# Eight convolution products per attention step in place of ten, and the first projection item begun in the last steps

## The reference

```python
def short_conv(u, b_gate, c_gate, w):
    z = jnp.pad(c_gate * u, ((0, 0), (CONV_W - 1, 0), (0, 0)))
    y = z[:, 0:s_len] * w[0]
    for i in range(1, CONV_W):
        y = y + z[:, i:i + s_len] * w[i]
    return b_gate * y

def hybrid_mixer(h, w_in, ...):
    z = h @ w_in                      # q, keys, values, gates, u, bg, cg
    ...
    o_attn = g[0] * o_cmp + g[1] * o_sel + g[2] * o_win    # 8 heads of 64
    o_conv = short_conv(u, bg, cg, conv_w)                 # 512 channels
    return jnp.concatenate([o_attn, o_conv], axis=-1) @ w_o

h = layer_norm(ALPHA * h + hybrid_mixer(h, ...), ln1_g[l], ln1_b[l])
```

## Time and profile before

| what | value |
|---|---|
| median of 3 runs | 2651.23 us (2649.49 to 2657.9) |
| profiled execution, its own time | 2649.5 us |
| its span, first to last instruction | 2647.6 us |
| mean granted clock of TensorE | 0.977 |
| TensorE busy | 2498.7 us, 94% |
| VectorE busy | 1392.4 us, 53% |
| ScalarE busy | 1035.5 us, 39% |
| steps 0 to 34 of mixer 2 | 1149.58 to 1290.48 us of the span |
| steps 0 to 34 of mixer 3 | 1821.95 to 1964.47 us of the span |

### The profile page before, as it was taken

The page is one execution under the profiler, slowest core; times in us unless marked ns, Lnnn a source line. Parts: engine busy times, 40 slices in busy tenths (PEclk is TensorE's granted clock), DMA queues, the critical chain, the costliest instruction groups (busy, mean ns, idle before and its releaser), DMA issues.

```text
span 2647.6 us, 37963 instructions
## 1 busy us (share of the span) xinstructions
PE 2498.7 (94%) x15190; PEld 2009.3 (76%) x15190; DVE 1392.4 (53%) x2043; ACT 1035.5 (39%) x1402; POOL 192.8 (7%) x136
## 2 busy tenths in 40 slices
PE   7999999998999999999999999998987999999993
PEld 5888888776788887877668888777765878887872
DVE  3433446465443345466463323456655666666666
ACT  4222233334322223345442212234544556555652
POOL 1000010000100002200130000220002000000000
PEclk9999999999999999999999999999998999999997
DMA  4232223201222221321112322222113677777773
GB/s 146 101 109 80 107 85 111 71 26 40 104 103 103 80 107 68 107 96 49 48 64 95 112 81 105 83 91 96 49 39 153 237 266 269 274 270 267 273 261 133
DMA packets 50752, 328.36 MB, mean 124 GB/s; under 512 B 5857, under 2 KB 5985, under 8 KB 19169
## 3 DMA queue, kind: packets, MB, share of 16 engines
q1 hardware_dynamic: 45184, 310.60, 32.5%
q0 software_dynamic: 4032, 13.88, 1.4%
q10 hardware_dynamic: 1440, 2.57, 0.3%
HBM read 317.58 MB, written 9.44 MB: 124 GB/s over the span
## 4 chain that ended last, share of the span: by engine, by line
PE 85%; DVE 7%; ACT 3%; DMA 2%; issue 2%; POOL 1%; ACTq 0%; DVEq 0%; SPq 0%; POOLq 0%
PE ps L2285 16%; PE ps L2286 16%; PE ps L2287 16%; PE ps L912 5%; PE ps L1515 3%; PE ps L1501 3%; PE ps L1516 3%; PE ps L1517 3%; PE ps L1558 2%; PE ps L1544 2%; PE ps L417 1%; PE ps L1560 1%; PE ps L1559 1%; PE ps L967 1%; PE ps L1002 1%
## 5 line engine op out<-in xcount | busy, mean ns | idle before, releaser
L2285 PE MATMUL ps<-xh,wh 128*128 128x512 f32 x1344 | 532.4, 396 | 37.3 <-DVE xl L2141 14.0
L2286 PE MATMUL ps<-xl,wh 128*128 128x512 f32 x1344 | 528.4, 393 | 0.0
L2287 PE MATMUL ps<-xh,wl 128*128 128x512 f32 x1344 | 528.2, 393 | 0.0
L1877 DVE TENSOR_TENSOR wl<-raw,wh 128x2048 fp32r<-128x2048 f32 (+3 forms) x137 | 330.1, 2410 | 151.5 <-ACT wh L1872 151.5
L1872 ACT CAST wh<-raw 128x2048 fp32r<-128x2048 f32 (+3 forms) x137 | 270.1, 1972 | 326.0 <-PE ps L2287 291.4
L1733 DVE TENSOR_TENSOR wml<-raw_m,wmh 128x2048 fp32r<-128x2048 f32 (+1 forms) x146 | 307.0, 2115 | 118.4 <-ACT wmh L1593 117.7
L2285 PEld LDWEIGHTS ps<-xh,wh 128*128 128x128 f32 x1344 | 256.1, 191 | 96.5 <-issue 23.9
L1593 ACT CAST wmh<-raw_m 128x2048 fp32r<-128x2048 f32 (+1 forms) x146 | 257.6, 1770 | 106.7 <-PE ps L1501 73.0
L2286 PEld LDWEIGHTS ps<-xl,wh 128*128 128x128 f32 x1344 | 255.8, 190 | 54.7 <-issue 1.5
L2287 PEld LDWEIGHTS ps<-xh,wl 128*128 128x128 f32 x1344 | 255.5, 190 | 53.9
L2285 PE MATMUL ps<-ah,wh 128*128 128x512 f32 x528 | 206.2, 391 | 0.0
(11 more groups left out here) (379 smaller groups left out, 3946.0 us busy)
## 6 DMA issues: line engine op xcount, KB each, us to landing
raw_m<-in_moe SPq DMA_DIRECT2D x104, 1024.0 KB, 5.2
raw<-in_ffn_up SPq DMA_DIRECT2D x65, 1024.0 KB, 4.8
raw_m<-in_moe SPq DMA_DIRECT2D x32, 768.0 KB, 4.2
raw<-in_in SPq DMA_DIRECT2D x20, 1024.0 KB, 4.9
raw<-in_ffn_down SPq DMA_DIRECT2D x12, 1536.0 KB, 6.5
raw<-in_ffn_down SPq DMA_DIRECT2D x12, 1280.0 KB, 5.3
raw<-in_cmp SPq DMA_DIRECT2D x8, 1024.0 KB, 4.7
raw<-in_out SPq DMA_DIRECT2D x8, 1024.0 KB, 4.7
```

Source lines behind the costliest of these rows:

```text
L1877: nc.vector.tensor_tensor(wl[:, slot, 0:size], raw[:, slot, 0:size], wh[:, slot, 0:size].bitcast(F32), ALU.subtract).then_inc(lo_ready, 1)
L2285: nc.tensor.matmul(dst, hi_w, hi_x, start=(k == 0), stop=False)
L2286: nc.tensor.matmul(dst, hi_w, lo_x, start=False, stop=False)
L2287: return nc.tensor.matmul(dst, lo_w, hi_x, start=False, stop=(k == last_k))
```

## The change

- DENSE is 8, so that the 240 products fill steps 0 to 29; chunk_end and all that is placed by it move with them.
- The convolution results are split one by one, ScalarE in steps 22, 25, 28 and 31 (chunk_end(8 + c) + 2), VectorE one step later each (23, 26, 29, 32), and go to the unused ends of the weight slots (conv_part) in place of xh and xl. ScalarE's wait for the last convolution item is gone.
- 15 of the 48 products of the projection's item 0 (units 0 to 4 of 16, three products each) are issued within the steps: one unit in step 30, one in 31, one in 32, two in 34, each time between the scores (where there are any) and the transposes. In step 30 a wait for the item's split weights (lo_ready) and for the evacuation of the last convolution item (evac_done) stands ahead of them. The other 33 follow the steps.
- Item j of the projection uses banks 0 and 1 for even j and 4 and 5 for odd j, in both mixers.

```diff
--- before.py
+++ after.py
@@ -58,7 +58,7 @@
 TILES = (0, 1, 2, 3)
 STEPS = 8 * NT
 STEPS1 = 4 * NT
-DENSE = 10
+DENSE = 8
 WIN = 4 * NCMP
 TILE = P * P // P
 UPS = 12
@@ -318,6 +318,11 @@
             "h_att", "h_masked", "h_turned", "h_ktok", "h_upd", "h_state", "h_out", "h_sq", "h_stat", "h_rstd", "h_rec"))
         MIX0 = split_base["mixed0"]
         MIXED_ORDER = (4, 5, 6, 7, 0, 1, 2, 3)
+        EARLY = ((30, 0, 1), (31, 1, 2), (32, 2, 3), (34, 3, 5))
+
+        def conv_part(w, c):
+
+            return w[:, c // 2, ITEM + (c % 2) * S:ITEM + (c % 2 + 1) * S]
         turned = reset
         x_free, qk_hi, qk_lo, p_half, p_evac, h_hi, h_lo = (sem(n) for n in (
             "x_free", "qk_hi", "qk_lo", "p_half", "p_evac", "h_hi", "h_lo"))
@@ -888,7 +893,7 @@
 
             return ((q - 2) * 24 + 23) // DENSE if q >= 2 else -1
 
-        def pe_mixer(pe, l):
+        def pe_mixer(pe, l, mixed_early):
             n0, nb = first[f"cmp{l + 1}"], first[f"conv{l + 1}"]
             u0, t0 = STEPS1 + STEPS * l, NT * l
 
@@ -1017,6 +1022,7 @@
                     scores(s)
                 for x in range(s * DENSE, min((s + 1) * DENSE, 240)):
                     conv(2 + x // 24, x % 24, x % 24 + 1)
+                mixed_early(l + 1, s)
                 if 0 <= s - 2 < STEPS:
                     turn(s - 2)
                 if 8 <= s < 12:
@@ -1116,10 +1122,10 @@
                             half_split(nb + k + 1, h)
                 if s >= 13 and (s - 13) % 8 == 0 or s == STEPS + 3:
                     out_hi((s - 11) // 8)
-                if 26 <= s < 30:
-                    act.wait_ge(item_done, nb + 6)
-                    act.wait_ge(v_conv, 4 * l + s - 25)
-                    nc.scalar.copy(xh[:, 4 + s - 26], cy[:, s - 26]).then_inc(x_hi, 1)
+                for c in range(4):
+                    if s == chunk_end(8 + c) + 2:
+                        act.wait_ge(v_conv, 4 * l + c + 1)
+                        nc.scalar.copy(conv_part(wh, c), cy[:, c]).then_inc(x_hi, 1)
 
         def dve_mixer(dve, chain, l):
             na, n0, nb = (first[f"{name}{l + 1}"] for name in ("in", "cmp", "conv"))
@@ -1316,10 +1322,10 @@
                             half_split(nb + k + 1, h)
                 if s >= 13 and (s - 13) % 8 == 0 or s == STEPS + 3:
                     out_lo((s - 11) // 8)
-                if 26 <= s < 30:
-                    c = s - 26
-                    dve.wait_ge(x_hi, base + c + 1)
-                    nc.vector.tensor_tensor(xl[:, 4 + c], cy[:, c], xh[:, 4 + c].bitcast(F32), ALU.subtract).then_inc(x_lo, 1)
+                for c in range(4):
+                    if s == chunk_end(8 + c) + 3:
+                        dve.wait_ge(x_hi, base + c + 1)
+                        nc.vector.tensor_tensor(conv_part(wl, c), cy[:, c], conv_part(wh, c).bitcast(F32), ALU.subtract).then_inc(x_lo, 1)
 
         def cs_flat(g):
             return cs[:, g].rearrange("p i c n -> p (i c n)")
@@ -2229,7 +2235,7 @@
                         dve.wait_ge(n_bias, KD * (2 * l - 1))
                     if j == 3:
                         norm_shift(norm_name, ALPHA)
-                    add_to_x(n, n % 2, j, ALPHA, 1.0)
+                    add_to_x(n, j % 2, j, ALPHA, 1.0)
                 norm(norm_name, n)
 
             dve.wait_ge(vecs_loaded, 16)
@@ -2354,31 +2360,48 @@
                         norm_end(norm, n)
                 item_loop(pe, first[stage], count, step, peel_first=True)
 
+            def mixed_products(l, n, units):
+
+                slot, bank = n % 2, 4 * ((n - first[f"out{l}"]) % 2)
+                for m, i, k in units:
+                    if n == first[f"out{l}"] and m == 0:
+                        if k >= 4:
+                            pe.wait_ge(x_lo, split_base[f"mixed{l}"] + i + 1)
+                        if k == 0:
+                            pe.wait_ge(o_lo, NT * l)
+                    hi_x, lo_x = (conv_part(wh, k - 4), conv_part(wl, k - 4)) if k >= 4 else (qh[:, k], ql[:, k])
+                    tile = slice((m * KD + k) * TILE, (m * KD + k + 1) * TILE)
+                    mm = split_product(ps[:, bank + m], wh[:, slot, tile], wl[:, slot, tile], hi_x, lo_x, i, KD - 1)
+                return mm
+
+            first_units = [(m, i, k) for i, k in enumerate(MIXED_ORDER) for m in range(2)]
+
+            def mixed_early(l, s):
+
+                n = first[f"out{l}"]
+                if s == EARLY[0][0]:
+                    pe.wait_ge(lo_ready, n + 1)
+                    pe.wait_ge(evac_done, n)
+                for at, a, b in EARLY:
+                    if s == at:
+                        mixed_products(l, n, first_units[a:b])
+
             def mixed_columns(l, norm):
 
-                def step(n, slot, half, j):
+                for j in range(4):
+                    n = first[f"out{l}"] + j
+                    if j == 0:
+                        mixed_products(l, n, first_units[EARLY[-1][2]:]).then_inc(item_done, 1)
+                        continue
                     wait_item(n)
-                    eager = j == 0
-                    if not eager:
-                        order = [(m, i, k) for m in range(2) for i, k in enumerate(MIXED_ORDER)]
-                    else:
-                        order = [(m, i, k) for i, k in enumerate(MIXED_ORDER) for m in range(2)]
-                    for m, i, k in order:
-                        if j == 3 and (m, i) == (1, 0):
+                    for m in range(2):
+                        order = [(m, i, k) for i, k in enumerate(MIXED_ORDER)]
+                        if j == 3 and m == 1:
                             norm_middle(norm)
-                        if eager and m == 0 and k >= 4:
-                            pe.wait_ge(x_lo, split_base[f"mixed{l}"] + i + 1)
-                        if eager and m == 0 and k == 0:
-                            pe.wait_ge(o_lo, NT * l)
-                        hi_x, lo_x = (xh[:, k], xl[:, k]) if k >= 4 else (qh[:, k], ql[:, k])
-                        tile = slice((m * KD + k) * TILE, (m * KD + k + 1) * TILE)
-                        mm = split_product(ps[:, 4 * slot + m], wh[:, slot, tile], wl[:, slot, tile], hi_x, lo_x, i, KD - 1)
+                        mm = mixed_products(l, n, order)
                     mm.then_inc(item_done, 1)
                     if j == 3:
                         norm_end(norm, n)
-                for j in range(4):
-                    n = first[f"out{l}"] + j
-                    step(n, n % 2, n // 2, j)
 
             def tokens(n, width):
 
@@ -2416,12 +2439,12 @@
             ffn("ffn2", "ffn2", FF, "ln_in")
             columns("in1", 4, KD, xh, xl, x_lo, split_base["ln_in"])
             tokens(first["tok1"], 280)
-            pe_mixer(pe, 0)
+            pe_mixer(pe, 0, mixed_early)
             mixed_columns(1, "ln1_0")
             ffn("ffn3", "ln1_0", 2 * FF, "ln2_0")
             columns("in2", 4, KD, xh, xl, x_lo, split_base["ln2_0"])
             tokens(first["tok2"], 280)
-            pe_mixer(pe, 1)
+            pe_mixer(pe, 1, mixed_early)
             mixed_columns(2, "ln1_1")
             pe_moe(pe)
```

## The result

| | median | runs | ratio to before |
|---|---|---|---|
| before | 2651.27 us | 10 (2646.98 to 2657.9) | |
| after | 2660.77 us | 10 (2656.1 to 2665.49) | 1.0033, 95% interval 1.0021 to 1.0044 |

What follows compares the result with a forecast made beforehand. TensorE, with 6.8 us idle per mixer behind step 24 as all the change could go after. Terms summed to +0.2 us (mixer 2) and -1.5 (mixer 3), together -1.3: 2648.2 on the profiled execution, 2649 as median; range 2639 to 2656.

Steps and rivals of the forecast that it cites:

- Steps 24 to 29: 48 products land here and the waits go: 28.3 us against 21.38, +6.9 us per mixer.
- Steps 30 to 34: A 4.7 us TensorE wait is added in step 30; 23.0 us in all, +6.2 in mixer 2, +4.5 in mixer 3.
- Rival 1: The wait in step 30 is only 3.2 us and the clock holds: -7 to -10 us, 2641; chance 0.22.
- First item: First projection item: 15 fewer products, -3.5 us per mixer; the next item's weights stay hidden.
- Steps 0 to 23: Two fewer products per step give -10.7 us, 1.1 and 0.2 given back: net -9.4 us per mixer.
- The wait for a mask at step 6: TensorE reaches step 6 about 2.4 us earlier and waits some 1.1 us for VectorE's mask.
- step 13: Taps, a half split and the low part of the first result tile meet here; charged 0.2 us.
- 2 (VectorE the bound in steps 8 to 23): Shorter steps 8 to 23 are not got; with half the 9.4 kept, +9.4 for both mixers, 2657.6 us; chance 0.09.
- 3 (the mix of transposes lowers the clock, full products keep it up whatever the wait): Full products in steps 24 to 34 hold 2.4 GHz; +1.5 us in each mixer goes, 2646; chance 0.14.
- 4 (the early products of step 30 fill nothing): TensorE waits for their bank first; already the forecast for step 30, no separate chance; steps 31, 32, 34 do fill waits.

Runs made afterwards that it cites:

- i1: Kernel after with VectorE's last convolution output one step earlier (step 29) and its half splits one step later for all but the first pair; 0.9954 of before.
- e1: Ten products per step as in before and no early products, but convolution results split where the change puts them; 0.9986 of before.
- h1: Kernel after with only VectorE's work on the last convolution output moved one step earlier, to step 29; 0.9974 of before.
- f1: Kernel after with nine products per step in place of eight, early products kept; 0.9958 of before.

## Why the prediction was wrong

Sum of the forecast: mixer 2 +0.2, mixer 3 -1.5. Measured from step 0 to the norm: +3.7 (194.87 against 191.21) and +1.5 (193.64 against 192.11). That is 6.5 us more than forecast, and about 4 more by the medians are the open rest. The last line of the sum has a slip besides: 2648.2 + 1.7 is 2649.9, not 2649. By its steps:

- **Steps 24 to 29: right.** 28.3 forecast, 28.08 measured in both, no waits left.
- **Steps 30 to 34: right, with its mechanism.** 4.7 us of idle forecast in front of the first early product, 4.74 measured in both mixers; 23.0 us forecast, 23.57 and 23.22 measured. VectorE's order was as it had been written out, to the normalisation and the gate product. Rival 1, the cheap wait, did not hold.
- **First item: nearly.** Its 15 products (3.5 us) are gone from it and the second item's weights are in time. Together with the last steps +2.7 and +1.0 were forecast; the stretch from step 30 to the norm grew by 3.4 and 1.3. The second item starts 3.6 us later counted from the first scores (1308.96 - 1153.23 against 1301.69 - 1149.58), outside the 2 us that I had allowed.
- **Steps 0 to 23: the step that failed.** -9.4 forecast, -6.4 and -6.5 measured, 5.9 us for both mixers, nearly all of the 6.5. It is steps 8 to 23 that fell short: by the forecast's terms they should give 16 x 0.467 - 0.2 = 7.3 us, and they gave 4.4 in each mixer (71.21 to 66.84 in mixer 2). The 2.9 that are missing are the longer wait of step 8 (1.3) and the slow stretch behind it (1.7). The work did shrink as priced. The wait for a mask at step 6, for which I had charged 1.1, was 0.16 and 0.87. What failed is the sentence "the taps and splits a step later; VectorE has slack again (44.97 busy of 71.21)". Slack over 16 steps says nothing of one step in which 0.48 + 1.54 + 1.22 us of VectorE's work fall between two masks. I had looked at step 13 for such a meeting and put 0.2 us on it; the one that counted is in step 7, because in step 8 TensorE wants the copy that ScalarE makes in this same step (that of step 6) before it goes on, an extra wait that only steps 8 to 11 have. With the meeting undone (i1) steps 0 to 23 take 93.20 against 102.74, -9.5: the forecast's term.
- **The clock in steps 0 to 23** was not in the sum at all. Half-speed time there went from 3.4 to 10.2 us in each mixer of this pair. 3.4 of it stands behind the wait of step 8 and costs the 1.7 us above. The other 3.4 lies in steps 0 and 1 and costs little: in mixer 2 the stretch of step 1 is twice as long, but 1.5 us of it fall within the wait of 4.1 us, and steps 0 and 1 grow from 10.83 to 11.25 us; in mixer 3 the added stretch lies in step 0, where TensorE waits for VectorE anyway, and they shrink from 10.77 to 10.41. Nor is it shown to be the change's: the two further executions of before have 6.8 us there as well.

**The rivals.** 2 (VectorE the bound in steps 8 to 23) had the right sign and the right engine and the wrong extent: one step, not sixteen. 3 (the mix of transposes lowers the clock, full products keep it up whatever the wait) is refuted twice. The kernel after has the full products and a clock of 0.86 and 0.85 in its last steps. And e1 has none there, the same 108 matmuls as before with the same 32 transposes, and the full clock (steps 30 to 34 of both mixers, columns as above; its longest wait in them is 1.4 us, in before 1.8):

```profile
1273.70:1289.63 15.93, 12.72 (x108) 8.73 (x108) 7.69 (x25) 9.42 (x23) 0.00 (x0) 1.00 0.01 1
1942.89:1958.83 15.94, 12.74 (x108) 8.71 (x108) 7.71 (x25) 9.43 (x23) 0.00 (x0) 1.00 0.00 0
```

So the Trainium skill's rule that transposes do not count (TensorE: Matmul & The Clock Gate, Part 4: PE-mode transpose) does not by itself explain the slow tails. The Trainium skill's rule on idle gaps (same page, "Why this matters for your kernels") agrees in direction: with the wait of 4.7 us the last steps of mixer 2 have 0.86, without it (h1) 1.00. 4 (the early products of step 30 fill nothing) was the forecast and held; those of steps 31, 32 and 34 did fill waits: h1 has 0.4 us of wait left in its last steps, before had 4.2 in three waits. I had 0.08 on slower: the forecast stood at 2649 with one wait found by writing out one step, and nothing in the chances stood for a second wait of the same kind in a step that I had not written out.

## What to carry to other kernels

When work moves from one step to another in hand-ordered engines, write out each engine's queue for every step in which two moved pieces meet, and for every step that has an extra wait of its own; an average of busy time over many steps hides them. Before early work is put in front of a wait, ask where the releasing operation stands in the other engine's order. Here one operation of VectorE, 0.7 us long, moved one step ahead turned a loss of 0.3% into a gain of 0.3%, and a wait of TensorE cost 1.4 to 1.7 times its length because of the slow clock that came with it.

## What the runs showed of the hardware

- Short waits of TensorE can already bring a stretch at half clock (1.2 GHz). In step 8 of the profiles of eight per step a wait of 1.63 to 1.73 us was followed by one of 3.4 us in 13 of 16 cases; waits of 2.2 to 2.4 us in the last steps in 4 of 4; waits of 4.7 us came with one of 6.8 us in 8 of 8, which in after's mixer 2 begins 2 us before the wait ends. With 1.4 to 1.5 us (nine per step, f1) there was none in 2 cases, with 0.4 us in step 8 none in 18. In mixer 2 of before, the wait of 1.75 us that ends step 29 is followed by one at 1273.9 in this profile and not in the two further ones; in those a wait of 1.28 us in step 32 is followed by one, while e1 has 1.35 us at that place and none. In mixer 3 of the two further ones a stretch begins 0.2 to 0.3 us before the wait of 1.74 us ends. Length alone doesn't decide it for short waits.
- The cost of such a stretch is at most half its length and less where TensorE waits within it anyway: of the 6.8 us that come with the wait of step 30, 4.75 were busy, and the whole came to 7.1 - 4.7 = 2.4 us.
- The 2270 us outside mixers 2 and 3 scatter by up to 15 us between executions of one kernel, roughly with the clock, three times the effect in question; the two mixers together repeat within 0.6 us.
